# Where an mLSTM layer's modulation weights are multiplied in a two-block transformer kernel

## What is computed

```python
mod_l = split(silu(c) @ ada_w[i] + ada_b[i], 6)        # latent: 6 vectors of 1024
mod_c = split(silu(c_ctx) @ ada_w[i] + ada_b[i], 6)    # context
u  = rms_norm(h, norm_mix[i]) * (1 + mod_l[1]) + mod_l[0]
uc = rms_norm(hc, norm_mix[i]) * (1 + mod_c[1]) + mod_c[0]
y, yc = mixer(uc, u)                                   # block 2: i=0 mLSTM, i=1 window attention
h = h + mod_l[2] * y
a = rms_norm(h, norm_ffn[i]) * (1 + mod_l[4]) + mod_l[3]
h = h + mod_l[5] * (square(relu(a @ ffn_w1[i])) @ ffn_w2[i])
# the context tokens alike, except in the last layer of a block
```

## Time and profile before

| | |
|---|---|
| median of 3 runs | 2283.47 us (2281.47 to 2286.61) |
| profiled execution | 2282.79 us, its span 2281.0 us |
| mean granted clock of PE | 0.980 of full speed |
| PE busy | 2165.2 us, 95% |
| DVE busy | 1635.8 us, 72% |
| ACT, POOL busy | 886.2 us, 690.7 us |
| loaded from HBM | 338.04 MB, 149 GB/s over the span |

### The profile page before, as it was taken

The page is one execution under the profiler, slowest core; times in us unless marked ns, Lnnn a source line. Parts: engine busy times, 40 slices in busy tenths (PEclk is TensorE's granted clock), DMA queues, the critical chain, the costliest instruction groups (busy, mean ns, idle before and its releaser), DMA issues.

```text
span 2281.0 us, 31323 instructions
## 1 busy us (share of the span) xinstructions
PE 2165.2 (95%) x12512; PEld 1823.0 (80%) x12512; DVE 1635.8 (72%) x2368; ACT 886.2 (39%) x1345; POOL 690.7 (30%) x455
## 2 busy tenths in 40 slices
PE   6999999999999989998999889979999999999997
PEld 3887777788888778898988777757888887858997
DVE  6665667987677994867798876778877684685443
ACT  3323333222333342444444437633223333364453
POOL 0000210233344620203266333312333455213344
PEclk9999999999999999999999999989999999999999
DMA  9432234465655463354755542223665553614552
GB/s 321 141 102 74 65 103 157 129 199 172 206 180 188 162 200 102 122 176 147 232 185 176 175 139 65 75 77 124 207 200 169 202 181 78 141 38 133 182 185 74
DMA packets 268024, 341.14 MB, mean 150 GB/s; under 512 B 31056, under 2 KB 181464, under 8 KB 267624
## 3 DMA queue, kind: packets, MB, share of 16 engines
q1 hardware_dynamic: 266704, 334.92, 45.7%
q10 hardware_dynamic: 1176, 4.23, 0.6%
HBM read 338.04 MB, written 1.08 MB: 149 GB/s over the span
## 4 chain that ended last, share of the span: by engine, by line
PE 78%; DVE 12%; issue 3%; ACT 3%; POOL 2%; DMA 1%; SPq 0%; DVEq 0%; ACTq 0%; POOLq 0%
PE PS L718 22%; PE PS L720 21%; PE PS L719 21%; DVE bias L1777 4%; DVE w_l L1747 3%; PE PS L823 1%; PE PS L768 1%; PE PS L773 1%; PE PS L769 1%; PE PS L1141 1%; PE PS L958 1%; POOL a_l L2397 1%; DVE work L1877 1%; PE PS L967 1%; PE PS L981 1%
## 5 line engine op out<-in xcount | busy, mean ns | idle before, releaser
L718 PE MATMUL PS<-a_h,w_h 128*128 128x512 f32 (+1 forms) x2624 | 906.9, 346 | 21.0 <-DVE w_l L1747 11.8
L719 PE MATMUL PS<-a_l,w_h 128*128 128x512 f32 (+1 forms) x2624 | 895.0, 341 | 0.0
L720 PE MATMUL PS<-a_h,w_l 128*128 128x512 f32 (+1 forms) x2624 | 894.9, 341 | 0.0
L1747 DVE TENSOR_TENSOR w_l<-ring,w_h 128x1024 fp32r<-128x1024 f32 (+1 forms) x416 | 581.1, 1438 | 199.4 <-ACT w_h L1340 198.8
L1340 ACT ACTIVATE w_h<-ring 128x1024 fp32r<-128x1024 f32 (+1 forms) x416 | 409.0, 1033 | 536.9 <-PE PS L720 515.2
L718 PEld LDWEIGHTS PS<-a_h,w_h 128*128 128x128 f32 x2624 | 498.9, 190 | 108.2 <-issue 34.3
L720 PEld LDWEIGHTS PS<-a_h,w_l 128*128 128x128 f32 x2624 | 499.0, 190 | 56.4
L719 PEld LDWEIGHTS PS<-a_l,w_h 128*128 128x128 f32 x2624 | 499.4, 190 | 53.0
L1777 DVE SCALAR_TENSOR_TENSOR bias<-ring,silu,bias 128x512 f32<-128x512 f32 x504 | 430.0, 904 | 4.5 <-DMA ring<-in_w_mod 0.5
L2397 POOL TENSOR_TENSOR a_l<-hid,a_h 128x2048 fp32r<-128x2048 f32 (+1 forms) x60 | 231.3, 3855 | 233.4 <-ACT a_h L1364 233.4
L2412 POOL TENSOR_TENSOR hid<-hid 128x256 f32<-128x256 f32 (+1 forms) x128 | 156.8, 1226 | 417.1 <-ACT hid L1322 417.1
(11 more groups left out here) (221 smaller groups left out, 2569.8 us busy)
## 6 DMA issues: line engine op xcount, KB each, us to landing
ring<-in_w_ff SPq DMA_DIRECT2D x64, 1024.0 KB, 6.1
ring<-in_ffn_w SPq DMA_DIRECT2D x64, 1024.0 KB, 5.4
ring<-in_w_mod SPq DMA_DIRECT2D x48, 1024.0 KB, 5.2
ring<-in_ada_w SPq DMA_DIRECT2D x48, 1024.0 KB, 5.2
ring<-in_w_in SPq DMA_DIRECT2D x42, 1024.0 KB, 5.4
ring<-in_mlstm_w_in SPq DMA_DIRECT2D x12, 1024.0 KB, 7.2
ring<-in_w_o SPq DMA_DIRECT2D x8, 1024.0 KB, 5.3
ring<-in_w_attn_out SPq DMA_DIRECT2D x4, 1024.0 KB, 5.4
```

Source lines behind the costliest of these rows:

```text
L718: nc.tensor.matmul(out, stat[0], mov[0], start=start, stop=False, **kw)
L719: nc.tensor.matmul(out, stat[0], mov[1], start=False, stop=False, **kw)
L720: return nc.tensor.matmul(out, stat[1], mov[0], start=False, stop=stop, **kw)
L1747: V.tensor_tensor(w_l[:, n % 2, c], ring[:, split_raw[n] % SLOTS, c], w_h[:, n % 2, c].bitcast(F32), ALU.subtract).then_inc(s_wl, 1)
```

## The change

Layer 2's blocks 2 to 8 (14 tiles) now lie in layer 1's feed-forward: seven in ff1 at steps 1, 3, ..., 13 and seven in ff2 at steps 0, 2, ..., 12, each whole in its step. Their transposes come at ff1's steps 3, 7, 11 and ff2's 0, 4, 8, 12 (before: 6 and 14 in each). m_in holds block 9 alone, whose halves are multiplied at steps 3 and 4, behind the split of the step; its transposes come at step 4 (before at 2 and 4). m_out has none. The gate scans go to steps 1 and 2. In m_out's first step PE takes head 7's mean square after chunk 2. The ring's slots are no longer t mod 4: each tile takes the slot that is given back first in DVE's order, and the transfers are issued in the order in which their slots are given back, which turns out to be the order of the tiles as before. The numbers of compute instructions are the same on every engine, as is the number of transfers.

```diff
-            st["mods"], mods = mods[:count(i)], mods[count(i):]
+            if at is None or i in at:
+                st["mods"], mods = mods[:per], mods[per:]
...
-            if i in carry:
-                full, carried = [], full
-            elif carried:
-                full, carried = carried, None
...
-            phase("m_in", tiles=(1,) + (2,) * 4 + (4,), halves=(0,), mods=blocks(2, 6, 8), at=range(1, 5), **base)
+            phase("m_in", tiles=(1,) + (2,) * 4 + (4,), halves=(0,), mods=blocks(2, 9, 10), at=(3, 4), **base)
-            phase("to_h", tiles=(2,) * 4, src="m", gate=2, name="m_out", mods=blocks(2, 8, 10),
-                  per={0: 2, 1: 1, 2: 1}, carry=(0,), **base)
+            phase("to_h", tiles=(2,) * 4, src="m", gate=2, name="m_out", **base)
...
-        spread = layer == 1
+        spread = False
-            1: (blocks(2, 2, 4), range(1, 16, 4), blocks(2, 4, 6), range(1, 16, 4)),
+            1: (blocks(2, 2, 5) + [(2, 5, 0)], range(1, 15, 2), [(2, 5, 1)] + blocks(2, 6, 9), range(0, 14, 2)),
...
-        SPLIT_FIRST = (("ff1", 1), ("m_in", 1), ("m_in", 3))
+        SPLIT_FIRST = (("ff1", 1), ("m_in", 3), ("m_in", 4))
...
+        given_back = {mod_raw[key]: i for i, key in enumerate(sorted(mod_raw, key=mod_raw.get)[:8])}
+        def give_back(t):
+            if t is not None:
+                given_back.setdefault(t, len(given_back))
+        for ph in plan:
+            if ph["kind"] == "norm" and not ph["final"]:
+                give_back(split_raw[ph["s"]])
+                give_back(split_raw[ph["s"] + 1])
+            for st in ph["steps"]:
+                after = None if st["s"] is None else split_raw.get(st["s"] + 1)
+                if split_before_mods(ph, st):
+                    give_back(after)
+                for key, ks in st["parts"]:
+                    if ks[-1] == 3:
+                        give_back(mod_raw[key])
+                give_back(after)
+        slot_of, follows, holder = [], [], [None] * SLOTS
+        for t in range(len(tiles)):
+            slot = min(range(SLOTS), key=lambda i: -SLOTS + i if holder[i] is None else given_back[holder[i]])
+            slot_of.append(slot)
+            follows.append(holder[slot])
+            holder[slot] = t
+        order = sorted(range(len(tiles)), key=lambda t: -len(tiles) + t if follows[t] is None else given_back[follows[t]])
...
-                for t in range(sent[0], upto):
-                    if t >= SLOTS:
-                        what, count, _ = stream[t - SLOTS]
+                for t in order[sent[0]:upto]:
+                    if follows[t] is not None:
+                        what, count, _ = tiles[follows[t]]
...
-                            for ks in (range(0, 6), range(6, 8)):
+                            for ks in (range(0, 3), range(3, 8)):
...
-                            act.wait_ge(s_mcsum, ph["mu"] + 2)
+                            act.wait_ge(s_mcsum, ph["steps"][4]["modu"] + 1)
...
-                        if i in (2, 4):
-                            scan_rows(i // 2 - 1)
+                        if i in (1, 2):
+                            scan_rows(i - 1)
```

More of the change, by code:

```diff
@@ L70, in add_units, with phase @@
             n["u"] += 1
-    def phase(kind, tiles=(), units=0, mods=(), per=1, at=None, splits=0, extra=None, banks=(0, 1, 2, 3), halves=(), spread=False, carry=(), **kw):
+    def phase(kind, tiles=(), units=0, mods=(), per=1, at=None, splits=0, extra=None, banks=(0, 1, 2, 3), halves=(), spread=False, **kw):
         ph = dict(kind=kind, norm=n["norm"], head=n["head"], x=n["x"], s=n["s"], u=n["u"], mu=n["mu"], **kw)
         mods = list(mods)
-        steps, rest, carried = [], None, None
-        count = (lambda i: per.get(i, 0)) if isinstance(per, dict) else (lambda i: per if at is None or i in at else 0)
+        steps, rest = [], None
         for i, e in enumerate(tiles):
-            st = dict(s=n["s"] if e is not None else None, u=n["u"], units=e or 0, mods=[], modu=None, modkey=None, parts=[], late=False,
+            st = dict(i=i, s=n["s"] if e is not None else None, u=n["u"], units=e or 0, mods=[], modu=None, modkey=None, parts=[], late=False,
                       half=i in halves, extra=(extra or {}).get(i, ()))
@@ L456, in push_mods @@
                 w = io["w_mod" if layer < 2 else "ada_w_2"][layer % 2]
-                mod_raw[key] = len(stream)
+                mod_raw[key] = len(tiles)
                 if key not in by_pe:
-                    what, count = "mod", 1 + sum(x[0] == "mod" for x in stream)
+                    what, count = "mod", 1 + sum(x[0] == "mod" for x in tiles)
                 else:
                     what, count = "mod_pe", b + half + 1
-                stream.append((what, count,
+                tiles.append((what, count,
                                [(lambda t: view4(t), rows(w[512 * half:512 * half + 512, 512 * b:512 * b + 512]))]))
@@ L467, in push_split @@
             if s < len(split_src):
-                split_raw[s] = len(stream)
-                stream.append(("split", 2 * s + 2, split_src[s]))
+                split_raw[s] = len(tiles)
+                tiles.append(("split", 2 * s + 2, split_src[s]))
         push_mods([(0, b + up, half) for b in (0, 2) for half in range(2) for up in (1, 0)])
@@ L479, in build, with split_before_mods @@
                 push_split(0)
+        def split_before_mods(ph, st):
+            return st["late"] or (ph["kind"], st["i"]) in SPLIT_FIRST and (ph["layer"] == 1 or ph["kind"] == "m_in")
+        given_back = {mod_raw[key]: i for i, key in enumerate(sorted(mod_raw, key=mod_raw.get)[:8])}
[21 more added lines that the diff above has]
+        order = sorted(range(len(tiles)), key=lambda t: -len(tiles) + t if follows[t] is None else given_back[follows[t]])
+        sent_at = {t: i for i, t in enumerate(order)}
         landed, total = [], [0] * SLOTS
-        for t, (_, _, parts) in enumerate(stream):
-            total[t % SLOTS] += 16 * len(parts)
-            landed.append(total[t % SLOTS])
+        for t, (_, _, parts) in enumerate(tiles):
+            total[slot_of[t]] += 16 * len(parts)
+            landed.append(total[slot_of[t]])
         release, inner = [], 0
@@ L503, in raw_slot @@
         def raw_slot(eng, t):
-            eng.wait_ge(s_slot[t % SLOTS], landed[t])
-            return ring[:, t % SLOTS, :]
-        mod_count = {key: stream[t][1] for key, t in mod_raw.items()}
+            eng.wait_ge(s_slot[slot_of[t]], landed[t])
+            return ring[:, slot_of[t], :]
+        mod_count = {key: tiles[t][1] for key, t in mod_raw.items()}
         def wait_units(eng, n):
@@ L591, in build @@
                 for key in st["mods"]:
-                    if key[2] == 0 and before is not None and key[:2] not in ((0, 3), (2, 9)):
+                    if key[2] == 0 and before is not None and key[:2] != (0, 3):
                         mod_before[key] = before
@@ L599, in acc_of @@
         def acc_of(key):
-            return second_acc if key[:2] in ((0, 3), (2, 9)) else acc
+            return second_acc if key[:2] == (0, 3) else acc
         def mod_vectors(key):
@@ L1754, in split_half @@
                 dve.wait_ge(s_wh, 2 * n + i + 1)
-                V.tensor_tensor(w_l[:, n % 2, c], ring[:, split_raw[n] % SLOTS, c],
+                V.tensor_tensor(w_l[:, n % 2, c], ring[:, slot_of[split_raw[n]], c],
                                 w_h[:, n % 2, c].bitcast(F32), ALU.subtract).then_inc(s_wl, 1)
@@ L1815, in steps_of @@
                 for i, st in enumerate(ph["steps"]):
-                    if (ph["kind"], i) in SPLIT_FIRST and (ph["layer"] == 1 or ph["kind"] == "m_in") or st["late"]:
+                    if split_before_mods(ph, st):
                         split_w(st["s"] + 1)
```

16 lines of the change are left out of this document (8 added, 8 removed).

## The result

The changed kernel takes 2270.18 us in the median (2269.76 to 2271.02, 4 runs) against 2282.47 (2281.26 to 2286.61, 4 runs): a ratio of 0.9945, interval 0.9932 to 0.9958. The profiled execution has a span of 2267.9 us, 13.1 less than before.

The account below looks back on a forecast made before the run. TensorE carries 78% of the chain that ended last, with each touched stage having its own limit. Terms -17.0 - 5.5 + 3.5 + 18 + 2 - 0.3 = +0.7 gave 2284 us, no measurable change; range 2271 to 2292.

Parts of the forecast that it names:

- m_out: mLSTM output projection: four tiles leave, the early mean square covers head 7's wait; stage 44.8 us, -17.0.
- What is late next: m_out: step 1's weight split, ready at 1513.6 before step 0 ends at 1514.7; nothing charged, 1 us without that cover.
- m_in: Stage before the heads, two tiles instead of four: one TensorE wait of some 5 us before the only transposes; -5.5.
- now meet the scans: m_in: GpSimd's squares and scaling, which met the first tile set, would delay VectorE's gate scans instead; +5 on VectorE's line.
- Clock: Half-clock matmuls behind longer TensorE waits in ff2 and before m_in's transposes; 0 to 4 us, taken as +2.
- ff2: Layer 1's second feed-forward product, seven tiles instead of four, VectorE and GpSimd taking turns; +18, between +6 and +22.
- The sum in turn: Layer 1's ff2: undisturbed VectorE and GpSimd durations added, 101.3 us against 103.49 measured, taken as the stage's pace.
- Rival A: Tiles hide beside TensorE's work in ff1 (+1.5) and ff2 (+8), no clock loss; total -12.5, 2271 us; chance 0.33.
- ff1: Layer 1's first feed-forward product, seven tiles instead of four, more VectorE work; +3.5, between 1 and 6.
- Slots: Ring slots by first return: transfers stay covered, a few loads in layers 0 and 2 start earlier; -0.3.
- B: VectorE and GpSimd fully in turn: ff1 +5, ff2 +22, clock +4, m_in -4; total +10, 2293 us; chance 0.20.
- C: m_out gives -10 instead of -17, head 7's chain or a weight tile late; total +8, 2291 us; chance 0.09.

Follow-up runs that it names:

- e7: Changed kernel with head 7's mean square back behind chunks 0 to 5 of m_out; 0.9962 of the kernel before, m_out 49.45 us.
- e8: Kernel before with only head 7's mean square moved behind chunks 0 to 2 of m_out; ratio 0.9982, m_out 57.23 us.
- e6: Changed kernel without GpSimd's final norm of the first block's latents in m_in, but for one column; 0.9942 of the kernel before, m_in 66.26 us.
- e2: Kernel before without GpSimd's final norm of the first block's latents in m_in, but for one column; ratio 0.9966, m_in 72.45 us.
- e1: Kernel before with the new choice of ring slots alone, no tile, transpose or scan moved; ratio 0.9999.
- e4: Changed kernel without the multiplications of three ff2 tiles, (2,5,1), (2,6,1), (2,7,1), but for one column each; 0.9927 of the kernel before, ff2 116.72 us.
- e9: Changed kernel without the multiplications of three other ff2 tiles, (2,6,0), (2,7,0), (2,8,0), but for one column each; 0.9928 of the kernel before, ff2 116.06 us.

## Why the prediction was wrong

- **m_out** was right in mechanism and size: 44.64 us against 44.8. "What is late next", the split, had its cover; e7 and e8 confirm the two parts.
- **m_in** is the step that failed: "GpSimd's squares and scaling ... now meet the scans (5, ...)" and with it "TensorE ... then waits once for some 5 us". GpSimd does meet the scans, and costs VectorE 4.3 us in all, 3.4 of them in the scans (e6), so the 5 alone was no bad estimate. But it was added to rows of before that had GpSimd in them already. The first scan, two splits and the second set of sixteen were kept at their old lengths, and against e2's rows these hold 4.2 us of GpSimd, 2.6 of them in the second set. The changed kernel has nothing of this in the second set: 0.67 us for each L1804, while one GpSimd instruction stands for 12.46 us. I had taken it that the two engines alternate instruction by instruction wherever both have work, as they do in both sets of before. So GpSimd was charged with 9.2 us and cost 4.3. The last tile ends 7.5 us earlier relative to the stage's start (52.0 against 59.5), not 2.4, TensorE waits for nothing, and the stage comes out at -10.8 instead of -5.5. That is 5.3 of the 13.8 us by which the sum was off, the largest single part. What decides whether the engines alternate or one stands still, no run shows.
- **Clock**: +2 was charged, nothing of it is found as a sum. In ff2 it did fall (0.98 to 0.91), but the cost is inside that stage's 15.3. Elsewhere it came out 3.8 and 1.5 us lower and 1.5 us higher, in stretches that the change does not touch: the chance of a single profile. The medians carry less of it. The 3.5 us at the start are a quarter of what the sum was off by and have no cause in the change that e1 would show.
- **ff2** came out 2.7 us under its term, for a wrong reason. "The sum in turn, which matches the length of before" was an agreement of totals, not a mechanism: in the changed kernel it gives 117 and the stage takes 118.8, and yet e4 and e9 remove 16 us from the sum and 2 to 3 from the time. The rows spoke against it beforehand: such a bound allows no time in which neither engine works, and the earlier trace rows show VectorE idle for 11.7 us in that stretch; during more than 4 of them GpSimd is idle too. Besides, the sum left out 6 us of VectorE's other instructions there. What sets the stage's pace in its place is shown in part only: in steps 2 to 5 the delay of a split by a whole tile and the half clock behind it. Rival A priced the tiles at +8, far too low.
- **ff1** was right within its range of 1 to 6: 3.8 against 3.5 in this pair of profiles, some 2 over all.
- **Slots** gave nothing (e1), as charged.
- Rival A came nearest in time (2271) with its mechanism wrong: the tiles did not hide in ff2; m_in gave what ff2 did not. B's clock and m_in terms did not come, and C's wait in m_out did not either, with 1 us to spare where 0.7 was forecast.
- On the Trainium skill's rule of exclusion ("SBUF — State Buffer", "Who interferes with whom"): the traces agree that one engine blocks the other (one L2394 took 12.46 us, until VectorE's fourteen were through; without GpSimd's work VectorE was 7 us faster in e2), and in the tiles of m_in the one that pays was not the one that I charged.

## What to carry to other kernels

When VectorE and GpSimd exclude each other, find out for each stretch who gives way and whether anyone waits for that one. And when a row of the old profile is carried into a forecast, ask first what disturbance it already holds, or the disturbance is charged twice. A matching sum of two engines' work proves nothing while either of them still idles: leave some of that work out before believing it. Side work ahead of a just-in-time instruction should be priced by the block in front of it and by what the other engines do meanwhile, not by its total: seven whole tiles took 3.5 us more than the same seven in halves, and one whole tile, in the pause behind another, cost nothing here (steps 4 and 5) and 5 us there (steps 8 and 9).

## What the runs showed of the hardware

Waits of TensorE of 3 to 4 us were followed by half-rate matmuls (0.21 instead of 0.12 us from start to start for 256 columns): steps 3 of ff2 took 10.0 and 10.9 us at clock 0.66 and 0.59 (e4 and the changed kernel), of which the wait inside the step is 1.65. And where the half clock falls differs between profiles of kernels that are identical up to that point, by up to 4 us over the first 1050 us. A difference of 2 us in one stage of one profile is therefore no finding.

VectorE's 128x512 instructions with two inputs and GpSimd's 128x256 ones alternated in m_in before (fourteen in 11.71 us instead of 9.55). In the same stage of the changed kernel the same kinds of instruction did not: VectorE's ran at full pace and one of GpSimd's took 12.46 us, against 0.61 undisturbed for a square of the same size.
